# Transposed probability tiles of the last attention stage as one stream in runs of four

## The reference, cut to what matters

```python
kg = ksb[bi, gi, ib]           # selected branch: 8 of 16 blocks of 64 keys, per query
p = jax.nn.softmax(jnp.where(dist >= 0, scs, NEG), axis=-1)
o_slc = jnp.einsum('bqgrk,bqgkd->bqgrd', p.astype(vg.dtype), vg)
...
o_win = banded_attention(q, kw, vw, C_WINDOW, slopes)    # window of 512 keys
return gates[..., 0:1] * o_cmp + gates[..., 1:2] * o_slc + gates[..., 2:3] * o_win
```

## Time and profile before

| | |
|---|---|
| median of 3 runs | 872.6 us (870.66 to 873.0) |
| profiled execution, first to last instruction | 867.2 us |
| the stage of the change | about 540 to 761 us of it |
| PE, DVE, ACT busy over the span | 786.8, 571.2, 426.7 us |
| instructions | 16180 |

### The profile page before, as it was taken

How to read it: one execution, slowest core, us unless ns; L and a number is a source line. 1 busy time by engine, 2 the same in 40 slices (tenths; PEclk the granted TensorE clock), 3 DMA queues, 4 the chain that set the end, 5 groups by cost and what they waited for, 6 DMA issues and landing times. The chain is left out here.

```text
span 867.2 us, 16180 instructions
## 1 busy us (share of the span) xinstructions
PE 786.8 (91%) x6290; PEld 664.0 (77%) x6290; DVE 571.2 (66%) x1334; ACT 426.7 (49%) x966; POOL 113.7 (13%) x61
## 2 busy tenths in 40 slices
PE   4899999996988889877989998989998999989996
PEld 4899987685777767756868887778877888878885
DVE  6961111035789899847755997899998988943332
ACT  5631111113556565626743322778888888822221
POOL 0000000002000000002105421123110332132220
PEclk9999999998999999969998999899999999989999
DMA  7220125243232323134134431500001111034421
GB/s 293 103 86 38 37 98 154 77 112 111 67 104 68 104 67 98 55 92 134 49 87 137 122 86 41 146 2 1 3 2 51 50 51 50 2 122 146 146 98 48
DMA packets 31788, 72.34 MB, mean 83 GB/s; under 512 B 5088, under 2 KB 13664, under 8 KB 30688
## 3 DMA queue, kind: packets, MB, share of 16 engines
q1 hardware_dynamic: 31712, 71.31, 26.8%
HBM read 55.04 MB, written 16.25 MB: 82 GB/s over the span
## 5 line engine op out<-in xcount | busy, mean ns | idle before, releaser
L1645 ACT ACTIVATE n_probs<-n_probs,n_negated_max 128x640 f32<-128x640 f32 (+7 forms) x128 | 94.2, 736 | 28.4 <-DVE n_negated_max L1714 28.1
L1723 DVE SCALAR_TENSOR_TENSOR n_probsT_low<-n_turned,n_probsT_high 128x512 f16<-128x512 f32 (+3 forms) x192 | 94.4, 520 | 16.8 <-ACT n_probsT_high L1655 14.1
L706 PE MATMUL n_turned<-identity,n_probs 128*128 128x128 f32 x528 | 82.9, 281 | 6.3 <-ACT n_probs L1645 4.3
L1655 ACT ACTIVATE n_probsT_high<-n_turned 128x512 f16<-128x512 f32 (+3 forms) x192 | 80.7, 454 | 12.2 <-PE n_turned L706 11.8
L1817 PE MATMUL n_scores<-w_and_keys_high,stacks 128*128 128x256 f32 (+2 forms) x192 | 75.2, 392 | 5.5 <-DVE n_negated_max L1714 3.4
L706 PEld LDWEIGHTS n_turned<-identity,n_probs 128*128 128x128 f32 x528 | 59.6, 142 | 24.1 <-ACT n_probs L1645 16.4
L1818 PE MATMUL n_scores<-w_and_keys_low,stacks 128*128 128x256 f32 (+2 forms) x192 | 61.9, 333 | 0.0
L620 PE MATMUL nat<-stacks,xT_high 128*128 128x256 f32 (+1 forms) x192 | 56.1, 292 | 2.3 <-issue 2.2
L621 PE MATMUL nat<-stacks,xT_high 128*128 128x256 f32 (+1 forms) x192 | 55.2, 287 | 0.0
L622 PE MATMUL nat<-stacks,xT_low 128*128 128x256 f32 (+1 forms) x192 | 55.1, 287 | 0.0
L180 PE MATMUL a_projected<-xT_high,w_and_keys_high 128*128 128x512 f32 x128 | 52.3, 409 | 0.7 <-ACT staged L189 0.7
(11 more groups left out here) (263 smaller groups left out, 2177.3 us busy)
## 6 DMA issues: line engine op xcount, KB each, us to landing
w_raw<-in_w_feat SPq DMA_DIRECT2D x23, 512.0 KB, 3.9
features<-staged SPq DMA_DIRECT2D x30, 256.0 KB, 2.5
a_raw<-features SPq DMA_DIRECT2D x36, 128.0 KB, 2.7
s_raw<-features SPq DMA_DIRECT2D x18, 256.0 KB, 4.1
branches_b_c<-in_x SPq DMA_DIRECT2D x8, 512.0 KB, 6.2
silu_gates<-staged SPq DMA_DIRECT2D x16, 256.0 KB, 2.0
gatesT<-silu_gates SPq DMA_DIRECT2D x8, 512.0 KB, 4.8
keys_and_w_out_raw<-in_w_out SPq DMA_DIRECT2D x4, 1024.0 KB, 5.2
```

The costliest lines, as they stand in the source:

```text
L706: mm = nc.tensor.transpose(dst[:, j, :], src[:, c:c + P], ident[:, :])
L1645: nc.scalar.activation(pr[:, n % PS, 0:w], pr[:, n % PS, 0:w], ACT.Exp, scale=-1.0, bias=nmax[:, hb % 4, qt:qt + 1], accum_out=sums[:, hb ...
L1655: nc.scalar.activation(pth[:, g % GS, 0:k, :], tp[g % TS][:, 0:k, :], ACT.Copy, scale=PSCALE).then_inc(t_high, 1)
L1723: nc.vector.scalar_tensor_tensor(out=ptl[:, g % GS, 0:k, :], in0=tp[g % TS][:, 0:k, :], scalar=PSCALE, in1=pth[:, g % GS, 0:k, :], op0=ALU ...
```

## The change

All tiles of the stage, in the order of the units, are now one stream that is cut into runs of four: tile number t of the stream lies in run t // 4, slot t % 4. A unit's tiles are thus in pieces, and a run may hold tiles of two or three units. The class `TileRuns` holds the tables. 528 tiles make 132 runs, all of them full.

- `turn(n)` writes its pieces into the slots where the stream stands. It waits for a free bank only at slot 0, and tells ACT only when slot 3 is filled.
- `high_part(n)` and `low_part(n)` handle the runs that end in unit n: none, one or two, always 128x512.
- `values(n)` goes by pieces (220 in all) and waits for the `low_part` of each piece's run. That run may end in a later unit.
- The waits on counts are adapted: a bank of `n_probsT` is free when the last piece in it was used; `add_bias(n)` waits until the run with the last tile of unit n - 4 is full.

The work of PE is the same: 528 transposes and 1584 products. The order of the loops is untouched.

Where a unit's last tile ends up, by the tables: in 40 units the last run ends in the unit itself, in 80 in the next unit, in 8 in the unit after next. The 8 are units 6 and 14 of every 32 (6, 14, 38, 46, 70, 78, 102, 110), each a unit of 5 tiles before a unit of 1.

```diff
--- before.py
+++ after.py
@@ -718,6 +718,36 @@
     return mm
 
 
+class TileRuns:
+
+
+
+    def __init__(self, tiles_of_unit):
+        self.first = [0]
+        for t in tiles_of_unit:
+            self.first.append(self.first[-1] + len(t))
+        self.pieces, self.pieces_before, self.pieces_at_end = [], [0], {}
+        for n, t in enumerate(tiles_of_unit):
+            own, at = [], 0
+            while at < len(t):
+                run, slot = divmod(self.first[n] + at, 4)
+                k = min(4 - slot, len(t) - at)
+                own.append((run, slot, t[at:at + k]))
+                at += k
+            self.pieces.append(own)
+            self.pieces_before.append(self.pieces_before[-1] + len(own))
+            for i, (run, _, _) in enumerate(own):
+                self.pieces_at_end[run] = self.pieces_before[n] + i + 1
+
+    def ended_by(self, n):
+
+        return range(self.first[n] // 4, self.first[n + 1] // 4)
+
+    def up_to(self, n):
+
+        return (self.first[n + 1] - 1) // 4 + 1
+
+
 def diff_phase(nc, sig, feat_dram, gate_dram, w_feat, xh, xl, ring, stacks, va, ya, yr, ident, bias, bias_in, dist_full,
                query_scale, lams, lam_size):
     UN = A_H * NT
@@ -1546,7 +1576,7 @@
     for n in range(UN):
         qt = QT_ORDER[n % NT]
         tiles.append(list(range(max(qt - 4, 0), qt + 1)) if n % HU < NT else list(range(qt + 1)))
-    runs, before = softmax_chunks(tiles)
+    runs = TileRuns(tiles)
     AHEAD = 2
     PS, TS, GS = 4, 3, 6
     GU = RC * HU
@@ -1646,13 +1676,11 @@
                                      bias=nmax[:, hb % 4, qt:qt + 1], accum_out=sums[:, hb % 4, qt:qt + 1]).then_inc(exped, 1)
 
             def high_part(n):
-                for i, run in enumerate(runs[n]):
-                    g = before[n] + i
+                for g in runs.ended_by(n):
                     act.wait_ge(turned, g + 1)
                     if g >= GS:
-                        act.wait_ge(valued, g + 1 - GS)
-                    k = len(run)
-                    nc.scalar.activation(pth[:, g % GS, 0:k, :], tp[g % TS][:, 0:k, :], ACT.Copy,
+                        act.wait_ge(valued, runs.pieces_at_end[g - GS])
+                    nc.scalar.activation(pth[:, g % GS, :, :], tp[g % TS][:, :, :], ACT.Copy,
                                          scale=PSCALE).then_inc(t_high, 1)
 
             exponentials(0)
@@ -1708,7 +1736,7 @@
                 if n == 0:
                     dve.wait_ge(win_in, 16)
                 if n >= PS:
-                    dve.wait_ge(turned, before[n + 1 - PS])
+                    dve.wait_ge(turned, runs.up_to(n - PS))
                 dve.wait_ge(scored, n + 1)
                 b = bw[:, CW - w:CW] if br == 0 else bf[:, S - w:S]
                 nc.vector.tensor_tensor_reduce(out=pr[:, n % PS, 0:w], in0=sc[n % 2][:, at:at + w], in1=b,
@@ -1716,12 +1744,10 @@
                                                accum_out=nmax[:, n // NT % 4, qt:qt + 1]).then_inc(biased, 1)
 
             def low_part(n):
-                for i, run in enumerate(runs[n]):
-                    g = before[n] + i
+                for g in runs.ended_by(n):
                     dve.wait_ge(t_high, g + 1)
-                    k = len(run)
-                    nc.vector.scalar_tensor_tensor(out=ptl[:, g % GS, 0:k, :], in0=tp[g % TS][:, 0:k, :], scalar=PSCALE,
-                                                   in1=pth[:, g % GS, 0:k, :], op0=ALU.mult,
+                    nc.vector.scalar_tensor_tensor(out=ptl[:, g % GS, :, :], in0=tp[g % TS][:, :, :], scalar=PSCALE,
+                                                   in1=pth[:, g % GS, :, :], op0=ALU.mult,
                                                    op1=ALU.subtract).then_inc(t_low, 1)
 
             def write_out(hb):
@@ -1729,7 +1755,7 @@
                 s = sums[:, hb % 4, :]
                 ch.link(nc.vector.reciprocal(s, s))
                 ch.link(nc.vector.tensor_tensor(s.unsqueeze(2), s.unsqueeze(2), gate_of(h, 2 - br), ALU.mult))
-                dve.wait_ge(valued, before[NT * (hb + 1)])
+                dve.wait_ge(valued, runs.pieces_before[NT * (hb + 1)])
                 if hb >= 2:
                     dve.wait_ge(added, hb - 1)
                 nc.vector.tensor_tensor(red[:, hb % 2, :, :], ov[hb % 2][:, :].rearrange("p (q d) -> p q d", q=NT),
@@ -1824,11 +1850,12 @@
 
             def turn(n):
                 pe.wait_ge(exped, n + 1)
-                for i, run in enumerate(runs[n]):
-                    g = before[n] + i
-                    if g >= TS:
+                for g, slot, run in runs.pieces[n]:
+                    if slot == 0 and g >= TS:
                         pe.wait_ge(t_low, g + 1 - TS)
-                    transpose_run(pe, nc, tp[g % TS], pr[:, n % PS, :], run, tiles[n][0], ident).then_inc(turned, 1)
+                    mm = transpose_run(pe, nc, tp[g % TS][:, slot:slot + len(run), :], pr[:, n % PS, :], run, tiles[n][0], ident)
+                    if slot + len(run) == 4:
+                        mm.then_inc(turned, 1)
 
             def values(n):
                 h, br, qt = place(n)
@@ -1836,12 +1863,12 @@
                 g_of = h // RC
                 if n % NT == 0 and hb >= 2:
                     pe.wait_ge(headed, hb - 1)
-                for i, run in enumerate(runs[n]):
-                    g = before[n] + i
+                for i, (g, slot, run) in enumerate(runs.pieces[n]):
                     pe.wait_ge(t_low, g + 1)
-                    values_run(nc, ov[hb % 2][:, HD * qt:HD * (qt + 1)], pth[:, g % GS], ptl[:, g % GS], run,
+                    part = slice(slot, slot + len(run))
+                    values_run(nc, ov[hb % 2][:, HD * qt:HD * (qt + 1)], pth[:, g % GS, part, :], ptl[:, g % GS, part, :], run,
                                lambda kt: vbs[:, kt, KV + g_of, :, :] if br == 1 else vw[:, kt, g_of, :, :],
-                               i == 0, i == len(runs[n]) - 1).then_inc(valued, 1)
+                               i == 0, i == len(runs.pieces[n]) - 1).then_inc(valued, 1)
 
             scores(0)
             scores(1)
```

## The result

The changed kernel takes 884.7 us (median of 4 runs, 883.2 to 886.1) against 872.8 us before: ratio 1.0161, with the 95% interval 1.0123 to 1.0199. The forecast was slower, 880 us. The way was right, and the loss of 11.9 us is 1.6 times the predicted 7.6.

The account below looks back on a forecast made before the run. PE was taken as pacemaker of the selected halves, in step with ACT and DVE in window halves; 3.0 + 2.7 + 6.3 - 2.4 - 2.0 = +7.6 us gave 880 us against 872.6, range 867 to 892.

Parts of the forecast that it names:

- The unit after next: In `values` at 8 units, PE waits for the low part of the unit after next: 3.0 + 2.7 us.
- The second kind: Units 14, 46, 78, 110, before a window half: PE waits 1.36 us each, 5.4 us, counted by half as 2.7.
- the first kind: Units 6, 38, 70, 102, before a selected half: PE waits 0.74 us each, counted in full as 3.0 us.
- The fourth units: Fourth unit of each window half: stalls of 0.88 (odd heads) and 0.70 us (even), 6.3 less 2.4 already waited.
- The other crossings: Remaining next-unit waits, about seven per two heads short of room, 0.38 us each: taken at nothing, 10.6 us without slack.
- The saving: 60 fewer copies and low parts: DVE 3.9 us, ACT 3.2 us less; 2.0 us gained, in window halves only.
- paced by DVE and ACT: Rival: DVE and ACT, not PE, pace the stage, so it gets faster, 866.6 us; chance 0.16.
- nothing is taken up: Rival: every stall counts in full, 25.3 us less 2.0, giving 896 us; chance 0.12.
- no change: Rival: stalls fall into time PE would wait for exponentials anyway, saving cancels the rest, 872 to 873 us; chance 0.19.
- The step from the span to the timed median: Timed median stands 5.4 us above the profiled span, taken as unchanged: span 874.8 makes 880.2 us.

Follow-up runs that it names:

- the waits alone: Kernel before with its 192 runs plus only the new waits of `values`, slightly stricter (a unit's last old run held whole): 884.8 us, ratio 1.0159.
- The 72 waits alone: Kernel before plus only the added next-unit waits of `values` outside the 8 fourth units of window halves: 877.4 us, ratio 1.0063.
- the lag of three: `values(n - 3)` for `values(n - 2)`, `write_out` one unit later, 8 float16 tile buffers: 873.9 us on the changed kernel, 874.2 us on the kernel before.
- the crossings keep out of the window halves: Changed kernel with runs closed at each unit border of a window half, crossing only in selected halves, 168 runs: 871.5 us, ratio 1.0001.
- the fourth units' waits: Kernel before plus only the 8 added waits of `values` at the fourth unit of each window half: 874.3 us, ratio 1.0051.
- early closed runs: Changed kernel with runs closed ahead of units 7 and 15 of every 32: 880.0 us; also closed behind each window half's fourth unit: 875.1 us.
- the fifth buffer: Changed kernel with 5 instead of 4 buffers for a unit's probabilities (`PS = 5`): 882.0 us, ratio 1.0133.

## Why the prediction was right, and what was mis-sized

**The way and the mechanism** were right: PE waits in `values` for low parts that came with the next or the next but one unit, at the named units; the waits alone, without the full runs, give a loss as large, and the full runs without the waits give at most 1.6 us of it.

**The unit after next**, 3.0 + 2.7 = 5.7 us: 5.4 in the stage alone, 4.6 when taken out of the changed kernel. The sum is right, its parts only roughly. The second kind, counted by half, cost 1.16 us of 1.36 in three places and nothing in the fourth, where PE before stood for a bias anyway; the first kind, counted in full, cost nothing in one place of four. That the half came out is in part luck.

**The fourth units**, 6.3 - 2.4 = 3.9 us: 5.6 alone with the stricter wait, 2.6 taken out of the changed kernel. The odd heads' stall was read right (0.9 for 0.88) and counted in full where the clock was undisturbed, without the 0.3 us that was to be taken up; the even ones' was half (0.38 for 0.70) and cost the stage nothing. So the size is near by errors that offset each other.

**The other crossings**, taken at nothing: this is the term that failed. The step said that "an exponential that comes later than PE takes most of them up", and that in the selected halves the low parts are ahead of PE. The 72 waits alone cost 7.6 us in the stage, of which up to 1.2 may be the clock's. In the trace of that kernel PE stops for 0.3 to 0.9 us at units 1, 15, 17, 21, 27 and 29 of nearly every 32, and for 1.1 to 2.2 us at four places of the stage. The places aren't those that had been read: at unit 48, the pattern for the term, PE waits neither there nor in the changed kernel. Units 15, 27 and 29 are in selected halves, where the low part had been thought to be early. Of the 10.6 us that the prediction held as the other end, some two thirds came. In the changed kernel's own trace 12.9 of the 27.4 us of waits for low parts are of this sort.

**The saving**, 2.0 us: at most 3.3 (the waits alone against the changed kernel). DVE's busy time fell by 4.2 us, near the 3.9 worked out, ACT's by 1.9 against 3.2. With the lag of three, where PE hardly waits for low parts, no gain from the saving shows at all. Of the Trainium skill's two sentences (Perfetto Trace Analysis, "Optimizing Scalar/DVE Operations") it was the one on breaking up instructions that held here; the 7.5 us for DVE and 3.1 for ACT, estimates from that section's overheads, stand against 4.2 and 1.9 here, and 6.6 and 4.0 between the two kernels with a lag of three.

**The sum** then reads 5.4 + 5.6 + 7.6, less 2.7 by which the three overlap, less 3.3: 12.6 us, the growth of the stage. Since the parts were measured with the stricter wait, the overlap is what was left over, and two of the parts hold stretches of lower clock, the split between fourth units, others and saving is good to some 3 us, not better.

Of the rivals, "paced by DVE and ACT" fell with the lag of three, "nothing is taken up" was too much (15 us of the new waits took the place of old ones), and no change was found only with the longer lag or where the crossings keep out of the window halves. The step from the span to the timed median, 5.4 us, was mistaken: a timed run stands about 2 us above its own span, and the rest was the profiled execution of before being shorter than the median one.

## What to carry to other kernels

Filling an instruction to its full width by taking work from the next step of a pipeline shortens the producer's engine and makes the consumer wait for that next step. Ask first how far the consumer is behind in the trace of before: start of the consumer's piece against the end of the instruction that it will need; here it read three stalls to 0.2 us (0.95 for 0.74, 1.3 for 1.36, 0.9 for 0.88) and missed two small ones (0.38 for 0.70, none for 0.38), since each stall moves the low parts behind it. Then do it for every piece and don't take the small ones at nothing; and what an engine saves counts only where that engine is what the others wait for.

## What the runs showed of the hardware

The clock can fall in one execution and not in another, after the same stretch of the same work. In the window half of head 1 PE stands for 1.89 us, waiting for a bias, in the kernel before as in the one with the fourth units' waits; up to there the two do the same in this half. The kernel before, the 4 us around the pause and what follows:

```profile
575.50:579.50 4.00, 1.87 (x24) 1.48 (x24) 3.62 (x16) 1.36 (x5) 0.00 (x0) 1.00 0.00 0
579.20:582.60 3.40, 3.18 (x41) 2.71 (x41) 3.33 (x11) 2.51 (x9) 0.73 (x1) 1.00 0.00 0
```

The kernel with the fourth units' waits:

```profile
577.10:581.10 4.00, 1.87 (x25) 1.53 (x25) 3.66 (x15) 1.36 (x5) 0.00 (x0) 1.00 0.00 0
581.20:584.60 3.40, 3.40 (x33) 3.34 (x32) 3.33 (x11) 2.51 (x8) 1.37 (x2) 0.51 0.00 0
```

With 1.87 us of PE in both, the clock stayed at its upper level in the first and was at its lower one (1.2 GHz) for 3.4 us in the second; the unit that PE then had in hand took 2.24 us instead of 1.55. Five of the twelve profiled executions have this dip in head 1 (the fourth units' waits, the 72 others, both kernels with early closed runs, and the kernel before with a lag of three), and seven don't.

In two executions the clock fell for 6.8 us in head 4, after 4 us in which PE was busy for 2.12 and 2.60 us (the second in the kernel with the fifth buffer); it cost 3.1 us each time. The changed kernel had 4 us with 2.48 us of PE at the same place and kept its clock. So a lone stall of one or two microseconds can cost more than itself, but not in each execution, and a difference of 1 to 3 us between two single stages has to be checked for it. Which of the timed executions had it can't be seen.
